# One block for query projection, selection and experts, with the first 64 expert gathers issued between the query tiles

## The reference, cut to what matters

```python
def peer_ffn(x, wq, sub_keys, u_tab, v_tab):
    q = (xf @ wq).reshape(t, PEER_HEADS, 2, PEER_DKEY // 2)
    scores = jnp.einsum("thpc,hpnc->thpn", q, sub_keys).astype(jnp.float32)
    s_top, i_top = lax.top_k(scores, PEER_TOPK)
    cand_s = (s_top[:, :, 0, :, None] + s_top[:, :, 1, None, :]).reshape(...)
    cand_i = (i_top[:, :, 0, :, None] * PEER_NKEYS + i_top[:, :, 1, None, :]).reshape(...)
    best_s, best_pos = lax.top_k(cand_s, PEER_TOPK)
    expert_idx = jnp.take_along_axis(cand_i, best_pos, axis=-1)
    gates = jax.nn.softmax(best_s, axis=-1)
    def chunk(args):
        xc, ec, gc = args
        u = jnp.take(u_tab, ec, axis=0)
        act = jax.nn.gelu(jnp.einsum("cd,chkd->chk", xc, u).astype(jnp.float32)) * gc
        vv = jnp.take(v_tab, ec, axis=0)
        return jnp.einsum("chk,chkd->cd", act.astype(vv.dtype), vv)
...
        x = layer_norm(DEEPNORM_ALPHA * x + f, ln2_g[l], ln2_b[l])
```

## Time and profile before

| what | value |
|---|---|
| device time, median of 3 runs | 3984.98 us (3984.53 to 3987.44) |
| the profiled execution | 3994.24 us, its span 3992.5 us |
| PE busy | 3445.3 us (86%) |
| DVE busy | 2213.4 us (55%) |
| POOL busy | 1589.9 us (40%) |
| ACT busy | 1210.9 us (30%) |
| mean granted clock of PE | 0.925 |
| gathers (software queue) | 536.90 MB, 73728 packets |

### The profile page before, as it was taken

The page is one execution under the profiler, slowest core; times in us unless marked ns, Lnnn a source line. Parts: engine busy times, 40 slices in busy tenths (PEclk is TensorE's granted clock), DMA queues, the critical chain, the costliest instruction groups (busy, mean ns, idle before and its releaser), DMA issues. The chain is left out here.

```text
span 3992.5 us, 43987 instructions
## 1 busy us (share of the span) xinstructions
PE 3445.3 (86%) x13568; PEld 2339.8 (59%) x13568; DVE 2213.4 (55%) x4411; ACT 1210.9 (30%) x2204; POOL 1589.9 (40%) x1088
## 2 busy tenths in 40 slices
PE   5999998899989999988999989857776777776776
PEld 4888675678868886755788867633332333332332
DVE  6635356443326554466333265686667676666666
ACT  3332225433323323145333233312222222222222
POOL 3446320244545455200444633324443444443442
PEclk8999997999999999969999999979898988888898
DMA  6536310123435454200233422239999999999997
GB/s 236 191 112 241 128 64 1 43 90 98 164 124 192 137 204 172 85 11 15 86 99 125 164 75 59 75 157 422 422 422 379 422 422 378 422 422 379 421 422 327
DMA packets 141386, 839.01 MB, mean 210 GB/s; under 512 B 15824, under 2 KB 16464, under 8 KB 63952
## 3 DMA queue, kind: packets, MB, share of 16 engines
q0 software_dynamic: 73728, 536.90, 32.4%
q1 hardware_dynamic: 67536, 300.56, 21.5%
HBM read 835.31 MB, written 2.10 MB: 210 GB/s over the span
## 5 line engine op out<-in xcount | busy, mean ns | idle before, releaser
L254 POOL TENSOR_TENSOR wlo<-wraw,whi 128x1024 fp32r<-128x1024 f32 x357 | 907.0, 2546 | 1526.5 <-ACT whi L250 1526.3
L2097 PE MATMUL g_psF<-g_ring,g_diagb 128*128 128x512 f32 x1152 | 566.8, 655 | 299.8 <-ACT g_diagb L2075 299.8
L2097 PEld LDWEIGHTS g_psF<-g_ring,g_diagb 128*128 128x128 f32 x1152 | 240.7, 212 | 628.9 <-ACT g_diagb L2075 342.5
L261 PE MATMUL f_ps<-f_hh,whi 128*128 128x512 f32 x1408 | 552.4, 392 | 48.8 <-DVE f_hl L343 48.8
L250 ACT ACTIVATE whi<-wraw 128x1024 fp32r<-128x1024 f32 x357 | 377.5, 1058 | 688.2 <-DMA wraw<-in_wts 415.5
L262 PE MATMUL f_ps<-f_hl,whi 128*128 128x512 f32 x1408 | 551.4, 392 | 0.0
L263 PE MATMUL f_ps<-f_hh,wlo 128*128 128x512 f32 x1408 | 551.3, 392 | 0.0
L2034 DVE CUSTOM_DVE_ANT_0 g_prod<-g_ring,g_xrow 128x1024 f32<-128x1024 f32 x288 | 352.7, 1225 | 24.1 <-DVE gates L1912 14.5
L1985 POOL DMA_INDIRECT g_ring<-in_uv,g_ix x288 | 299.7, 1040 | 138.6 <-POOL g_ix L1980 78.0
L510 DVE TENSOR_TENSOR f_a<-f_sg,f_ps 128x512 f32<-128x512 f32 x88 | 60.5, 687 | 508.9 <-PE f_ps L263 486.7
L261 PEld LDWEIGHTS f_ps<-f_hh,whi 128*128 128x128 f32 x1408 | 266.7, 189 | 107.5 <-issue 52.0
(11 more groups left out here) (371 smaller groups left out, 5710.9 us busy)
## 6 DMA issues: line engine op xcount, KB each, us to landing
wraw<-in_wts SPq DMA_DIRECT2D x360, 512.0 KB, 3.5
m_wrow<-in_ada SPq DMA_DIRECT2D x52, 1024.0 KB, 6.9
m_erow<-in_ada SPq DMA_DIRECT2D x28, 1024.0 KB, 5.0
p_wt<-in_wtok SPq DMA_DIRECT2D x2, 3168.0 KB, 10.2
p_wt<-in_w SPq DMA_DIRECT2D x2, 3072.0 KB, 9.7
g_ring<-in_uv,g_ix POOLq DMA_INDIRECT x288, 17.1
g_low<-in_uv,g_ix POOLq DMA_INDIRECT x160, 22.1
xT<-in_xT SPq DMA_DIRECT2D x1, 2048.0 KB, 12.3
```

The lines of the kernel that those rows point to most:

```text
L254: self.nc.gpsimd.tensor_tensor(self.T.wlo[:, j % 4], self.T.wraw[:, j % 2], self.T.whi[:, j % 4].bitcast(F32), ALU.subtract).then_inc(self ...
L261: self.nc.tensor.matmul(out, hi, xh, start=first, stop=False)
L2097: mm = nc.tensor.matmul(psF[:, c], diag[:, s, k], vb[s][k][:, c * S:(c + 1) * S], start=False, stop=False, skip_group_check=True)
```

## The change

Both stages become one block, `peer`, written out without hardware loops.

- The first 64 gathers, 4 groups of the first token tile, use 6 slots that are free during the query stage. From query tile 5 on, each tile comes with three sets of two gathers. PE does half a query tile, a set, the other half, a set, the scores of the tile before, and a set. DVE does the dots of two sets, the selection of the new scores, the dots of the third set, and on every second tile a `choose`.
- During the query stage DVE selects for token tiles 0 and 1 alone. ACT keeps the scores of tiles 2 and 3 (`keep`, 16 copies), and DVE selects from them later (`kept`), two in each of 16 groups of the later part.
- The other 448 gathers have 15 slots. Nine of these lie on the query stage's buffers and wait until the last query tile is done. Each slot is given back by itself, after its own matmuls, and the gathers read `T.idx` directly, without the POOL copy of L1980.
- `psF` has two buffers, one for each of two token tiles, and `final(t)` runs inside the next token tile's groups. The closing matmuls with zeros (L2101) and the copies out of `psF` (L2046) are gone. `choose` is four groups ahead, without its first copy and without `passed`.

```diff
-def peer_keys(nc, T):
...
 def choose(nc, T, B, link, dve, M, n):
-    link(nc.vector.tensor_copy(B["tv"], T.topv[:, bass.ds(n * 2, 2)]))
...
-def peer_experts(nc, T):
...
+def peer(nc, T):
+    FIRST, PAIR, FOUR = 4 * TOP, 2, 4
+    LOW, TOPS, SPARE, OWN = 5, 4, 2, SLOTS_OWN
+    EARLY = OWN + SPARE
+    SLOT0 = 5
+    sets = [(j, PAIR) for j in range(0, FIRST, PAIR)] + [(j, FOUR) for j in range(FIRST, TOTAL, FOUR)]
+    ASETS = FIRST // PAIR
...
+                def gather(j):
+                    pool.wait_ge(M["h_pick"], j // TOP + 1)
+                    if earlier[j] is not None:
+                        pool.wait_ge(M["g_mm"], earlier[j] + 1)
+                    elif j < FIRST:
+                        if slot_of[j] >= LOW + TOPS + OWN:
+                            pool.wait_ge(M["e_x"], 2 * TT)
+                            pool.wait_ge(M["x_lo"], KD)
+                    else:
+                        pool.wait_ge(M["w_mm"], NQ2 + 4)
+                    nc.gpsimd.indirect_dma_start(...)
+                for n in (3, 4, 5, 6, 7):
+                    W.rest(pool, n // 4, n % 4)
+                for j in range(EARLY):
+                    gather(j)
+                for n in range(SLOT0, NQ2):
+                    if n + 3 < NQ2:
+                        W.rest(pool, (n + 3) // 4, (n + 3) % 4)
+                    for j in range(EARLY + 6 * (n - SLOT0), min(EARLY + 6 * (n - SLOT0) + 6, FIRST)):
+                        gather(j)
+                for j in range(FIRST, TOTAL):
+                    gather(j)
...
+            # tensor
+                W.pair(pe, psQ, xh, xl, M["x_lo"])
+                pe.wait_ge(M["g_al"], 1)
+                turn(0)
+                turn(1)
+                scores(0)
+                scores(1)
+                for n in range(2, NQ2 + 1):
+                    here = [s for s in range(3 * (n - SLOT0), 3 * (n - SLOT0) + 3) if 0 <= s < ASETS]
+                    if n < NQ2:
+                        query(n, 0)
+                    for s in here[0:1]:
+                        experts(s)
+                    if n < NQ2:
+                        query(n, 1)
+                    for s in here[1:2]:
+                        experts(s)
+                    if n >= 3:
+                        scores(n - 1)
+                    if n < SLOT0:
+                        turn(2 * n - 2)
+                        turn(2 * n - 1)
+                    for s in here[2:3]:
+                        experts(s)
+                for s in range(ASETS, len(sets)):
+                    experts(s)
...
+            # scalar
+                for n in range(3, NQ2 + 1):
+                    query(n - 1)
+                    if n + 3 < NQ2:
+                        W.round(act, (n + 3) // 4, (n + 3) % 4)
...
+                    for s in here[0:2]:
+                        weights(s)
+                    keep(n - 1)
+                    for s in here[2:3]:
+                        weights(s)
+                    if n % 2 == 0:
+                        exponents(n // 2 - 1)
...
+            # vector
+                for n in range(3, NQ2 + 1):
+                    for s in here[0:2]:
+                        dots(s)
+                        gated(s)
+                    fresh(n - 1)
+                    for s in here[2:3]:
+                        dots(s)
+                        gated(s)
+                    if n % 2 == 0:
+                        choose(nc, T, B, link, dve, M, n // 2 - 1)
+                for n in range(FIRST // TOP, GROUPS):
+                    if n + 4 < GROUPS:
+                        choose(nc, T, B, link, dve, M, n + 4)
+                    for i in range(4):
+                        dots(ASETS + 4 * (n - FIRST // TOP) + i)
+                        u = 2 * (n - FIRST // TOP) + i
+                        if i < 2 and u < 2 * NQ2:
+                            kept(u)
+                        gated(ASETS + 4 * (n - FIRST // TOP) + i)
+                        if i == 1 and n % PH == 0 and n >= PH:
+                            final(n // PH - 1)
+                final(TT - 1)
```

More of the change, by code:

```diff
@@ L1965, in peer_experts, with landed, _ @@
         ident = T.const[:, C_IDENT:C_IDENT + P]
+        def landed(eng, j):
+            eng.wait_ge(M["g_uv"][slot_of[j]], 16 * turn_of[j] + 16)
         with nc.Block() as block:
+            @block.sync
+            def _(sp):
+                W.ahead(sp=sp)
+                for n in range(4, NQ2):
+                    W.load(sp, n // 4, n % 4)
+                    if n == 5:
+                        sp.dma_start(keys[:, :, :], T.d["keys"]).then_inc(M["e_keys"], 16)
+                sp.wait_ge(M["e_sc"], NQ2)
+                sp.dma_start(lnp, T.d["ln2"]).then_inc(M["g_ln"], 16)
+                for t in range(TT):
+                    sp.wait_ge(M["g_fin"], t + 1)
+                    sp.dma_start(T.d["out"][t], r).then_inc(M["g_out"], 16)
+                sp.wait_ge(M["g_out"], 16 * TT)
@@ L2058, in exponents, with turned @@
+                def turned(n):
+                    t, half = divmod(n, 2)
+                    act.wait_ge(M["e_x"], n + 1)
+                    nc.scalar.activation(xtok[:, t, half * S:(half + 1) * S], psX[:, half], ACT.Copy).then_inc(M["e_xo"], 1)
                 def exponents(n):
@@ new lines, in weights @@
+                def weights(s):
+                    j0, size = sets[s]
+                    act.wait_ge(M["g_dot"], j0 + size)
+                    nc.scalar.activation(dot[:, s % 4, 0:size], dot[:, s % 4, 0:size],
+                                         ACT.Gelu_apprx_tanh).then_inc(M["g_gelu"], 1)
+                    act.wait_ge(M["g_w"], s + 1)
+                    if s >= 4:
+                        act.wait_ge(M["g_mm"], sum(sets[s - 4]))
+                    for k in range(size):
+                        nc.scalar.activation(diag[:, s % 4, k], ident, ACT.Copy,
+                                             scale=wgt[:, s % 4, k:k + 1]).then_inc(M["g_diag"], 1)
@@ new lines, in build @@
+                T.gates = s2("gates", [P, TT * PH, TOP])
+                T.rest = s2("e_rest", [P, 2, KEYS])
+                T.aid = s2("g_aid", [P, P])
+                small = 0
+                T.B = {}
+                for n, shape, t in (("ti", [2, TOP], F32), ("cand", [TOP * TOP], F32), ("rest", [TOP * TOP], F32),
+                                    ("best", [TOP], F32), ("pos", [TOP], U32), ("dif", [TOP], F32),
+                                    ("part", [2, TOP], U32), ("partf", [2, TOP], F32), ("eq", [2, TOP, TOP], F32),
+                                    ("key", [2, TOP], F32), ("sum", [1], F32)):
+                    T.B[n] = s2("h_" + n + "b", [P] + shape, t)[tuple([slice(None)] * (1 + len(shape)))]
+                    small += -(-math.prod(shape) // 8) * 8
```

501 lines of the change are left out of this document (226 added, 275 removed).

## The result

The changed kernel is slower: 4021.16 us (4019.25 to 4025.15, 4 executions) against 3985.18 us of before on the same chip, a ratio of 1.0091 with a 95% interval of 1.0073 to 1.0108. The forecast was 3986 us, no change, and its range ended at 4020. The profiled execution took 4025.15 us, its span is 4023.4 us; my sum gave 3993.5, so 30 us are missing.

A forecast was written before the change was run, and what follows sets the result against it. The prediction took PE to bound the query stage and DMA the expert stage at 422 GB/s. Its sum, +199.0 - 159.0 - 35.0 - 0.4 - 3.6 = +1.0 us, gave 3986 us, no measurable change; range 3960 to 4020.

The forecast's parts named there:

- The third set's wait: Query stage, each cycle: PE stands idle 6.7 us after the scores until the third set's dots and gates are done.
- the three changes of token tile: Late part: DMA's standstills of 11.66 us at each change between token tiles go away, 35.0 us saved.
- 64 gathers leave the late part: Stage bound by DMA: 64 gathers at 2.485 us move among the query tiles, 159.0 us saved.
- tile 4's scores: Start of the new query stage: PE is through two sets, half a tile and these scores at 2589.7 us.
- An even tile takes 28.8 us: Query stage, cycles with a `choose`: 27.6 us plus 1.2 for the subtraction's delay of the dots.
- The lock: Even tiles: POOL's 2.40 us subtraction and DVE's dots share an SBUF port pair; delay 0 to 2.4, taken as 1.2 us.
- the second idle: Even tiles: PE waits again, 2 us, for the next set's dots behind `choose`.
- the rival of longer cycles: Query stage: clock falls at even tiles' later wait too, costlier falls, subtraction's full 2.4 us; +22, 4008 us; chance 0.30.
- An odd tile: Query stage, cycles without `choose`: 6.7 us idle, 17.1 of PE work, 1.8 of clock loss, 25.6 us.
- 448 late gathers take 1113 us: Late part: the gathers left behind the query tiles run at 2.485 us each, DMA moving 422 GB/s without gaps.
- The rival of a late part that loses its pace: Late part: 15 slots, put-off selections and `final` cost one us in each of 28 groups; 4014 us; chance 0.08.
- PE sets the pace: Query stage: DVE's work is hidden, a cycle is 17.1 us, total 3885 us; chance 0.04.

The follow-up runs named there:

- e1_small_sub: POOL's subtraction for the weights of query tiles 8 to 15 cut to 64 of 1,024 columns, against the changed kernel; ratio to before 1.0043.
- padding: Satisfied waits written out on VectorE: added to the changed kernel, 4038.4 us (one execution); added where its late selections and `choose` are left out, ratio 1.0109.
- thinning: VectorE's late selections and `choose` left out, against the changed kernel; ratio to before 1.0076.
- the loop: Satisfied waits on VectorE executed as a loop: added to the changed kernel, ratio 1.0116; added where its late selections and `choose` are left out, 1.0075.
- ACT's padding: 32 satisfied waits added on ACT in each of the 112 late sets, against the changed kernel; 4025.0 us in one execution.

## Why the prediction was wrong

- **The pieces held.** The third set's wait is 6.49 us (6.7), `choose` takes 6.8 (7.0; its 14 waits at 0.12 us give back 1.7, not 1.5), the end after the last dot 18.7 (18.8), the three changes of token tile are gone, and the late part has no gap. That 64 gathers leave the late part was right. That tile 4's scores are done within 0.2 us of the forecast is luck: TensorE got the first set at 2576.2, 2.3 us early, and lost 2.1 of that again to the lower clock behind it (its matmuls took 6.47 us, not 3.6).
- **"An even tile takes 28.8 us" failed.** It took 31.7 in three cycles. The lock was paid in full (3.37 - 1.22 = 2.15 us, taken as 1.2), it pushed the second idle from 2 to 3.7 us, and in it the clock fell once more (6.32 instead of 3.67 us), which the sum had put at nothing. I had all of this in the rival of longer cycles and argued against it with the 2 us of idle, half of the 4 us that I had read in the earlier trace rows. But these 2 us left out half of the lock, and here the clock fell 2.2 us after the last matmul. `e1_small_sub` shows the mechanism. An odd tile took 26.35, 0.8 more than the sum: behind the first idle its eight matmuls took 6.6 to 6.7 us, so the lower clock cost nearly 3 us there, where the sum has 1.8 (on even tiles they took 5.4, as the sum has it). Together this is +9.7 us in nine cycles, +8 with the steps around them.
- **"448 late gathers take 1113 us" failed,** by 22 us, and this decided the verdict. It took the rate of the stage before, 422 GB/s, as the gathers' own. Two terms were missing. First, `ln2` and three outputs now run inside the saturated stage: 6.2 us by bytes, 4 to 7 measured. Second, one DMA engine falls behind by some 13 us (up to 14 it works alone at the end, less the 1 of before), because the written-out code of VectorE is fetched over it: padding, thinning and the loop move the stretch by about 1 us for a packet, and 15 packets at 0.97 us make 14.5. Both together are 17 to 20 of the 22 us; the 0.51 MB of code are another 1.2 us by bytes, and the rest is not told from how executions differ. The rival of a late part that loses its pace had the size for this (28 us) but another cause, slots and VectorE's list, and the trace shows neither.
- **"PE sets the pace" had 0.04,** for the list as written rightly. But I used it only as a rival. The sum itself said that a set stands ahead of the next tile; I didn't price moving it, and that is where the change's gain was.

## What to carry to other kernels

When work is woven into another engine's list, its place must be set by when its input is ready there, not by when it was issued: one place later in TensorE's list was worth 80 us here, the whole way from slower to faster. When a stage is bound by DMA, add up every byte that crosses it, code as well. Here the gathers were done when the latest of the 16 engines was, so writing out VectorE's loops had a price, about 1 us for 8 KB of code. In the changed kernel the averages over the stage hide it: DMA shows 421 GB/s throughout, and the price stands at the end of the stream, as a stretch with one engine busy.

## What the runs showed of the hardware that I had not expected

- VectorE's instructions in packets of 8 KB cost the stream of gathers about 1 us each (13.5 us for 14, 6.4 for 6, 6.6 for 7 fewer): 0.31 us for the packet itself and 0.66 for the gather's packet behind it. Why that one takes longer stays open, and so does why the packets of ACT's code have none such behind them and those of SP's a weaker one (0.72 us).
- ACT's padding gave a second late DMA engine beside the first (share 0.13 instead of 0.06), and the stretch did not grow (1138.5 us). What counts is the latest engine alone, so here the price of code depends on whose it is.
- The Trainium skill ("Runtime: NRT & Kernel Launch", "Instruction fetch mechanics") says that code is fetched by DMA in blocks ahead of execution, and that this is mostly hidden. It was hidden from VectorE, which waited for landings and not for issue, but not from the gathers that use the same DMA engine.
